# Weighted values of the attention in two TensorE passes with 128 stationary columns, in a streaming encoder step (Trainium2, one core)

## The reference, cut to what matters

```python
logits = jnp.where(mask, logits + decay, NEG)          # layer 0; layer 1 has no decay
p = jax.nn.softmax(logits, axis=-1).astype(v.dtype)
return jnp.einsum('bhqk,bkhd->bqhd', p, v)             # the weighted values
```

## Time and profile before

| what | value |
|---|---|
| median of 3 runs | 1653.4 us (1653.22 to 1656.17) |
| the profiled execution's own time | 1654.03 us |
| its span in the trace | 1652.2 us |
| PE, PEld busy | 1545.7 us (94%), 1457.5 us (88%) |
| DVE, ACT, POOL busy | 1110.3 us (67%), 727.6 us (44%), 428.2 us (26%) |
| steps of layer 0's attention | about 245 to 390 us of the span |
| steps of layer 1's attention | about 1029 to 1175 us |

### The profile page before, as it was taken

How to read it: one execution, slowest core, us unless ns; L and a number is a source line. 1 busy time by engine, 2 the same in 40 slices (tenths; PEclk the granted TensorE clock), 3 DMA queues, 4 the chain that set the end, 5 groups by cost and what they waited for, 6 DMA issues and landing times.

```text
span 1652.2 us, 30865 instructions
## 1 busy us (share of the span) xinstructions
PE 1545.7 (94%) x10826; PEld 1457.5 (88%) x10826; DVE 1110.3 (67%) x1965; ACT 727.6 (44%) x1492; POOL 428.2 (26%) x441
## 2 busy tenths in 40 slices
PE   4999979999979999999999897999987999999997
PEld 3787769998979999999998687999887999999997
DVE  4131038775878788888865236777587888888875
ACT  3312137775443343343344334777444334333424
POOL 1110024553332222222100002455233221222210
PEclk8999969999989999999999898999998999999999
DMA  7244531210121231232140447221012223312211
GB/s 261 87 137 136 150 99 49 58 40 26 52 77 54 100 102 62 90 102 71 56 144 11 170 144 209 79 64 33 26 52 77 65 89 102 102 52 101 102 51 58
DMA packets 127637, 146.06 MB, mean 88 GB/s; under 512 B 17761, under 2 KB 103841, under 8 KB 127569
## 3 DMA queue, kind: packets, MB, share of 16 engines
q1 hardware_dynamic: 127568, 145.16, 27.4%
HBM read 120.54 MB, written 24.60 MB: 88 GB/s over the span
## 4 chain that ended last, share of the span: by engine, by line
PE 80%; issue 6%; DVE 6%; ACT 3%; DMA 2%; POOL 1%; SPq 1%; POOLq 0%; DVEq 0%; ACTq 0%
PE ps L2009 26%; PE ps L1705 22%; PE ps L2040 20%; PE ps L1867 3%; PE ps L1911 2%; PE ps L1913 1%; PE ps L1912 1%; PE ps L1882 1%; PE ps L1890 1%; PE ps L1838 1%; POOL sacc L713 1%; DVE pre L1494 1%; DVE ptl L1347 1%; PE ps L1860 1%; DMA xn<-in_meta_tokens 0%
## 5 line engine op out<-in xcount | busy, mean ns | idle before, releaser
L1532 DVE TENSOR_TENSOR xT<-xT,ps 128x592 f32<-128x592 f32 (+1 forms) x256 | 194.9, 762 | 53.8 <-PE ps L2009 51.5
L814 POOL TENSOR_TENSOR ssum<-raw 128x512 f32<-128x512 f32 x32 | 43.1, 1347 | 486.2 <-DVE wul L1438 486.2
L2040 PE MATMUL ps<-bh,wuh 128*128 128x296 f32 (+1 forms) x512 | 154.5, 302 | 13.2 <-DVE wul L1438 8.2
L745 POOL TENSOR_TENSOR prob<-prob,rs 128x144 f32<-128x144 f32 (+4 forms) x160 | 118.8, 757 | 142.6 <-DVE rs L1337 142.6
L2040 PE MATMUL ps<-bl,wuh 128*128 128x296 f32 (+1 forms) x512 | 154.1, 301 | 0.0
L2040 PE MATMUL ps<-bh,wul 128*128 128x296 f32 (+1 forms) x512 | 153.8, 300 | 0.0
L1347 DVE TENSOR_TENSOR ptl<-ps,pth 128x256 fp32r<-128x256 f32 (+2 forms) x192 | 95.8, 500 | 67.8 <-ACT pth L970 67.7
L1705 PE MATMUL ps<-wh,xgh 128*128 128x512 f32 (+5 forms) x320 | 124.1, 388 | 11.5 <-issue 4.3
L1705 PE MATMUL ps<-wl,xgh 128*128 128x512 f32 (+5 forms) x320 | 122.8, 384 | 0.0
L1705 PE MATMUL ps<-wh,xgl 128*128 128x512 f32 (+5 forms) x320 | 122.6, 383 | 0.0
L2009 PE MATMUL ps<-hh,dn2h 128*128 128x296 f32 (+1 forms) x512 | 111.0, 298 | 0.0
(11 more groups left out here) (252 smaller groups left out, 4752.4 us busy)
## 6 DMA issues: line engine op xcount, KB each, us to landing
raw<-in_w_up SPq DMA_DIRECT2D x32, 1024.0 KB, 7.0
raw<-in_w_down SPq DMA_DIRECT2D x32, 1024.0 KB, 5.0
raw<-in_w_in_a SPq DMA_DIRECT2D x12, 1024.0 KB, 7.1
kv_mla<-stn SPq DMA_DIRECT2D x24, 256.0 KB, 2.2
raw<-in_w_o_a SPq DMA_DIRECT2D x8, 512.0 KB, 7.2
natk<-kv_mla SPq DMA_DIRECT2D x8, 512.0 KB, 3.5
raw<-in_w_o_b SPq DMA_DIRECT2D x8, 512.0 KB, 7.5
q_mla<-stn SPq DMA_DIRECT2D x16, 192.0 KB, 1.9
```

Of the source, the lines that this page charges most:

```text
L745: g.tensor_tensor(prob[c][0:rows, off:off + n], prob[c][0:rows, off:off + n], rs[0:rows, u:u + 1].to_broadcast([rows, n]), ALU.mult).then_ ...
L814: g.tensor_tensor(ssum[:, 1, :, :], a11, a21, ALU.subtract).then_inc(s_ready, 1)
L1532: v.tensor_tensor(a, a, two_banks(2 + m % 2, n), ALU.add).then_inc(x_ready if last else acc_done, 1)
L2040: i = te.matmul(ps[:, bank, 0:h], w[:, k, :], x, start=(u not in (3, 4, 6) and k == 0 and p == 0), stop=(k == 3 and p == 2), skip_group_ch ...
```

## The change

It joins the low and the high value tile of a head into one stationary operand of 128 columns (`vlh`, low first). One matmul of it with `pth` gives two results at once: in partitions 0 to 63 `vl*pth`, in partitions 64 to 127 `vh*pth`. A second matmul adds `vh*ptl` into partitions 0 to 63. So each block takes two matmuls instead of three, and the result lies in two halves of the partitions that still have to be added. ACT copies the upper half into `oh` as before and the lower half into a new tile `corr`; DVE subtracts `oh` from the upper half into `rest_`; POOL adds `rest_` and `corr` into `ol`, once per pair of heads over 128 partitions. ACT's and DVE's `out` move: ACT's behind `exp` 2, DVE's behind `row_max` 3. Part 0 of the weighted values waits for both copies; the copies of a pair's first head wait for POOL's addition of the pair before; `wo_first` waits for the additions instead of DVE's copies. `corr` and `rest_` lie in `sq`.

```diff
-        vh = at("vh", [P, 2, 7, P], F32R, R_G + 23552)
-        vl = at("vl", [P, 2, 7, P], F32R, R_G + 23552 + 7168)
+        vlh = at("vlh", [P, 2, 7, 2, 2, HD], F32R, R_G + 23552)
...
+        corr, rest_ = sq[:, 0, :], sq[:, 1, :]
...
+            g.memset(rst[:], 1.0).then_inc(o_sum, 1)
...
+                def add_parts(pair):
+
+                    pool.wait_ge(o_lo, pair * 2 + (H0 + 2))
+                    pool.wait_ge(o_corr, pair * 2 + (H0 + 2))
+                    g.tensor_tensor(ol[:, pair, :], rest_[:], corr[:], ALU.add).then_inc(o_sum, 1)
+
+                def head(h, c, pair=None):
+                    for u in range(4):
                         normalise(layer, h, c, u)
+                    if pair is not None:
+                        add_parts(pair)
+                    normalise(layer, h, c, 4)
...
                 for h in range(4):
-                    head(h, h % 2)
+                    head(h, h % 2, 0 if h == 3 else None)
                 with pool.Fori(0, PAIRS // 2 - 1) as i:
                     head_and_v(4 * i + 4, 0, 2 * i + 2, 0, i + 1)
-                    head(4 * i + 5, 1)
+                    head(4 * i + 5, 1, 2 * i + 1)
                     head_and_v(4 * i + 6, 0, 2 * i + 3, 1, i + 1)
-                    head(4 * i + 7, 1)
+                    head(4 * i + 7, 1, 2 * i + 2)
+                add_parts(PAIRS - 1)
...
                 def out(head, p, pair):
 
                     act.wait_ge(av_done, head + (H0 + 1))
-                    s.activation(oh[64 * p:64 * p + 64, pair, :], pf[0:HD, 3072:3072 + T],
-                                 ACT.Copy).then_inc(o_hi, 1)
+                    rows = slice(64 * p, 64 * p + 64)
+                    s.activation(oh[rows, pair, :], pf[HD:P, 3072:3072 + T], ACT.Copy).then_inc(o_hi, 1)
+                    if p == 0 and not (isinstance(pair, int) and pair == 0):
+                        act.wait_ge(o_sum, pair + (PAIRS * layer + 1))
+                    s.activation(corr[rows, :], pf[0:HD, 3072:3072 + T], ACT.Copy).then_inc(o_corr, 1)
...
-                        if u == 2 and not (isinstance(h, int) and h < 2):
-                            out(h - 2, c, pair - 1)
                         if not last:
                             qk(h, u, 1 - c)
                         exp(h, c, u)
+                        if u == 2 and not (isinstance(h, int) and h < 2):
+                            out(h - 2, c, pair - 1)
...
                     dve.wait_ge(o_hi, head + (H0 + 1))
-                    v.tensor_tensor(ol[rows, pair, :], pf[0:HD, 3072:3072 + T], oh[rows, pair, :].bitcast(F32),
+                    if p == 0 and not (isinstance(pair, int) and pair == 0):
+                        dve.wait_ge(o_sum, pair + (PAIRS * layer + 1))
+                    v.tensor_tensor(rest_[rows, :], pf[HD:P, 3072:3072 + T], oh[rows, pair, :].bitcast(F32),
                                     ALU.subtract).then_inc(o_lo, 1)
...
                     row_max(h, 2)
-                    if not (isinstance(h, int) and h < 2):
-                        out(h - 2, c, pair - 1)
                     recip(h, 1)
...
                     row_max(h, 3)
+                    if not (isinstance(h, int) and h < 2):
+                        out(h - 2, c, pair - 1)
...
                             pe.wait_ge(o_lo, head + H0)
+                            pe.wait_ge(o_corr, head + H0)
...
-                            te.matmul(out, vh[0:rows, vs, t, d], pr_h, start=(b == 0), stop=False, skip_group_check=True)
-                            te.matmul(out, vh[0:rows, vs, t, d], pr_l, start=False, stop=False, skip_group_check=True)
-                            te.matmul(out, vl[0:rows, vs, t, d], pr_h, start=False, stop=(b == 1), skip_group_check=True)
+                            te.matmul(pf[:, cols], vlh[0:rows, vs, t, p, :, :].rearrange("p s d -> p (s d)"), pr_h,
+                                      start=(b == 0), stop=False, skip_group_check=True)
+                            te.matmul(pf[0:HD, cols], vlh[0:rows, vs, t, p, 1, :], pr_l, start=False, stop=(b == 1),
+                                      skip_group_check=True)
...
-                        pe.wait_ge(o_lo, H0 + HEADS - 2)
+                        pe.wait_ge(o_sum, PAIRS * layer + PAIRS)
...
-                pe.wait_ge(o_lo, H0 + HEADS)
+                pe.wait_ge(o_sum, PAIRS * (layer + 1) + 1)
```

More of the change, by code:

```diff
@@ L230, in build @@
         op_hi, op_tmp, op_lo = sem("op_hi"), sem("op_tmp"), sem("op_lo")
+        o_corr, o_sum = sem("o_corr"), sem("o_sum")
         p_ps, snap_done, u11_done, u_add = (sem(n) for n in ("p_ps", "snap_done", "u11_done", "u_add"))
@@ L765, in split_v @@
                     src, r, t = views[0]
-                    g.tensor_tensor(vh[r, slot, NT, :].rearrange("p (h d) -> p h d", h=2), src.rearrange("p t h d -> p (t h) d"),
+                    g.tensor_tensor(vlh[r, slot, NT, :, 1, :], src.rearrange("p t h d -> p (t h) d"),
                                     ones[r, :].rearrange("p (h d) -> p h d", h=2), ALU.mult).then_inc(v_hi, 1)
                     for src, r, t in views[1:]:
-                        g.tensor_copy(vh[r, slot, t, :].rearrange("p t (h d) -> p t h d", h=2), src).then_inc(v_hi, 1)
+                        g.tensor_copy(vlh[r, slot, t, :, 1, :], src).then_inc(v_hi, 1)
                     pool.wait_ge(v_hi, j * 3 + 3 + 3 * PAIRS * layer)
@@ L772, in split_v @@
                 for src, r, t in (views[0:1] + views[2:3] if part == 1 else views[1:2]):
-                    i = g.tensor_tensor(vl[r, slot, t, :].rearrange("p t (h d) -> p t h d", h=2), src,
-                                        vh[r, slot, t, :].bitcast(F32).rearrange("p t (h d) -> p t h d", h=2), ALU.subtract)
+                    i = g.tensor_tensor(vlh[r, slot, t, :, 0, :], src, vlh[r, slot, t, :, 1, :].bitcast(F32), ALU.subtract)
                 if part == 2:
@@ L778, in attention @@
             def attention(layer):
-                def head(h, c):
-                    for u in range(5):
+                H0 = HEADS * layer
+                def add_parts(pair):
[4 more added lines that the diff above has]
+                    for u in range(4):
                         normalise(layer, h, c, u)
+                    if pair is not None:
+                        add_parts(pair)
+                    normalise(layer, h, c, 4)
                 def head_and_v(h, c, j, slot, turn):
@@ L1893, in weighted_v @@
                 def weighted_v(head, part, groups, pair, vs, p):
-                    d = slice(HD * p, HD * p + HD)
                     pe.wait_ge(g_lo, groups)
@@ L1908, in weighted_v @@
                             q0, q1 = max(first_q, P * max(b - 1, 0)), first_q + 256
-                            out = pf[0:HD, 3072 + q0:3072 + q1]
+                            cols = slice(3072 + q0, 3072 + q1)
                             pr_h, pr_l = ptv_h[0:rows, b, q0:q1], ptv_l[0:rows, b, q0:q1]
-                            te.matmul(out, vh[0:rows, vs, t, d], pr_h, start=(b == 0), stop=False, skip_group_check=True)
-                            te.matmul(out, vh[0:rows, vs, t, d], pr_l, start=False, stop=False, skip_group_check=True)
-                            te.matmul(out, vl[0:rows, vs, t, d], pr_h, start=False, stop=(b == 1), skip_group_check=True)
+                            te.matmul(pf[:, cols], vlh[0:rows, vs, t, p, :, :].rearrange("p s d -> p (s d)"), pr_h,
+                                      start=(b == 0), stop=False, skip_group_check=True)
+                            te.matmul(pf[0:HD, cols], vlh[0:rows, vs, t, p, 1, :], pr_l, start=False, stop=(b == 1),
+                                      skip_group_check=True)
                         return
                     for b, (t, rows) in enumerate(((5, P), (6, P), (NT, TX))):
-                        out = ps[0:HD, 7, 0:TX]
                         c0 = 2560 + TX * b
-                        te.matmul(out, vh[0:rows, vs, t, d], pth[0:rows, c0:c0 + TX], start=(b == 0), stop=False)
-                        te.matmul(out, vh[0:rows, vs, t, d], ptl[0:rows, c0:c0 + TX], start=False, stop=False)
-                        i = te.matmul(out, vl[0:rows, vs, t, d], pth[0:rows, c0:c0 + TX], start=False, stop=(b == 2))
+                        te.matmul(ps[:, 7, 0:TX], vlh[0:rows, vs, t, p, :, :].rearrange("p s d -> p (s d)"),
+                                  pth[0:rows, c0:c0 + TX], start=(b == 0), stop=False, skip_group_check=True)
+                        i = te.matmul(ps[0:HD, 7, 0:TX], vlh[0:rows, vs, t, p, 1, :], ptl[0:rows, c0:c0 + TX],
+                                      start=False, stop=(b == 2), skip_group_check=True)
                     i.then_inc(av_done, 1)
```

## The result

The changed kernel takes 1669.9 us (median of 5 runs, 1665.7 to 1680.1), the kernel before in the same session 1653.4 (5 runs, 1648.9 to 1656.2): ratio 1.0111, 95% interval 1.0071 to 1.0151. It is slower by 1.1%, clear of the spread of the runs. The profiled execution took 1669.92 us, its span is 1668.1 us, 15.9 more than before.

A forecast was written before the change was run, and what follows sets the result against it. It took a ring of waits through PE (some 90% loaded), ACT and DVE to bound each step. Loops -0.5 us plus tails 2 x 0.35 gave +0.2, so 1653.6 us for the median, range 1651 to 1656.5.

The forecast's parts named there:

- The failed step: ACT's two copies between `exp` 2 and `turned` 3: each was taken to cost 0.54 us, overlapping the next instruction.
- The forecast's two times, 296.98 and 297.00: Start of DVE's `turned` 3 closing a step: 296.98 in the new order, 297.00 in the old, so -0.02 us a step.
- ACT's copies cost their full length: Rival, between `exp` 2 and `turned` 3: copies don't overlap, 0.65 us each, 0.22 more a step; 1659 us, chance 0.15.
- The second miss: Rival, PE in the loops: added waits bring the granted clock to half in every third step; 1669 us, chance 0.05.
- the copy that DVE takes out of the way: DVE's copy moved behind `row_max` 3: counted, with PE's 0.47 us, as a gain that ACT's two copies take up.
- TensorE's gain: Parts 1 and 2 of the weighted values on PE: two matmuls a block instead of three save 0.47 us a step.
- the rival of the load that isn't hidden: Rival, PE's loads of 128 columns: each block pays 0.11 us more, ring closes 0.45 later; 1666 us, chance 0.05.
- DVE's wait ahead of `turned` 3: In each step, DVE idle for about 0.2 us before `turned` 3, released by ACT.
- part 0's end 0.2 us ahead of the transposes: Part 0 on PE, waiting for DVE's copy, was to end 0.15 us ahead of the end of `turned` 3.
- DVE sets the ring: Rival, loop steps: with ACT's copies under 0.42 us each, DVE decides, -0.27 us a step; 1647 us, chance 0.20.
- PE sets it all: Rival, whole loops: PE alone bounds, so its full saving of 23 us counts; 1631 us, chance 0.05.

The follow-up runs named there:

- split_high_first: Kernel split with the high part of the values in the first 64 stationary columns; 1647.76 us, ratio 0.9974 to the kernel before.
- places_back: Changed kernel with ACT's and DVE's copies back at their places before the change; 1651.32 us, ratio 1.0001 to the kernel before.
- split: Changed kernel with ACT's `oh` and DVE's copy at their old places, ACT's second copy left behind `exp` 2; 1648.76 us, ratio 0.9984 to the kernel before.
- fill: Changed kernel with the four matmuls of scores unit 4 given twice in every step; 1664.69 us, ratio 1.0085 to the kernel before.
- no_corr: Changed kernel without ACT's second copy, its terms left out of the result; 1655.41 us, ratio 1.0036 to the kernel before.
- after_free: Changed kernel, DVE's instruction reading `oh` twice, part 0 waiting for ACT's copies alone; 1668.36 us, ratio 1.0104 to the kernel before.
- dve_moved: Kernel before the change with DVE's copy alone moved behind `row_max` 3; 1664.24 us, ratio 1.0089 to the kernel before.
- act_back: Changed kernel with ACT's two copies alone back at their old place; 1671.81 us, ratio 1.0128 to the kernel before.
- best: split_high_first with the last head's low part added by DVE from PSUM, last projection taking `oh` products first; 1641.23 us, ratio 0.9936 to the kernel before.
- move_only: Kernel before the change, three passes and one ACT copy kept, both engines' copies at the new places; 1663.4 us, ratio 1.0074 to the kernel before.

## Why the prediction was wrong, step by step

*The failed step* is "A copy lasts 0.65 us and the next instruction starts about 0.11 before its end [...], so it costs 0.54". It rested on one row of an even head. After the change the way from `exp` 2 to `oh` is 0.71 us (1091.37 to 1092.08; forecast 0.58), from `oh` to the second copy 0.69 (forecast 0.54), from there to `turned` 3 0.56 (forecast 0.54, with this even head's overlap; in the next head, an odd one, 1102.71 to 1103.39, 0.68). That is 0.30 us more than in the sum in even heads and 0.42 in odd ones, and these copies are the term of the sum that was mis-sized. With the mean of the two on the forecast's step it would be 9.78 + 0.36 = 10.14; measured 10.02. The 0.1 between them is a second slip of the same kind. The forecast's two times, 296.98 and 297.00, belong to an even head's step, but its difference was set on the mean 9.80. From first transposes to first transposes (PE, before the change) an even head's step is shorter than an odd one's:

```profile
288.14 0.43 PE L1867 MATMUL ps<-cst,prob 128*128 128x128 f32 x2
...
297.81 0.43 PE L1867 MATMUL ps<-cst,prob 128*128 128x128 f32 x2
...
307.72 0.43 PE L1867 MATMUL ps<-cst,prob 128*128 128x128 f32 x2
```

The even one is 9.67 us, the odd one 9.91, for the odd head's copies lack the overlap before the change too. So the forecast for a step in the new order was really 9.67 - 0.02 = 9.65, and with the copies as measured it is 9.95 in even heads and 10.07 in odd ones, 10.01 in the mean. The rival "ACT's copies cost their full length" had the place and the price, at 0.22 us a step and a chance of 0.15, but not the cause: it thought of two engines that read the same PSUM columns, and split_high_first shows that the partitions decide. It gave 1659, and held no clock. That its 0.22 lies so near the measured 0.24 is luck: it left `oh` its overlap with the instruction ahead, and stood on the same mixed step.

*The second miss* is the clock. Nothing but the size of the waits spoke for or against it, and the rival had 0.05. It costs 5.6 us in the profiled execution. The two rivals came true together: 26 x 0.24 us and 5.6 on the forecast make 1665.4, where the changed kernel's runs begin (1665.7). As separate cases neither reached that. The rest up to the profiled execution's 1669.9 (the forecast for it was 1654.2) lies outside the loops, and no run takes it apart.

*A third step was wrong, and hidden by the first:* "the copy that DVE takes out of the way". DVE's copy was not taken out of the way. At the old place it stood where DVE has a wait anyway (for scores unit 3 at first, for `kh` once ACT has two copies there); at the new one it stands ahead of both `turned` 3 and part 0. The forecast compared the new order with the old kernel, never with the two passes in the old order, and so charged all of the loss to ACT. By the runs, in layer 1: 9.79, DVE's copy moved 10.13, ACT's too 10.17, two passes in place of three 9.75, the second copy 10.02. The other way round: two passes in the old order 9.53.

*Right:* TensorE's gain. From the start of parts 1 and 2 to the transposes behind them it was 1.65 us (298.88 to 300.53) and is 1.19 (1095.83 to 1097.02), 0.46 less, where 0.47 was forecast; with two passes the loads of PEld start like this:

```profile
1096.03 0.19 PEld L1929 LDWEIGHTS ps<-pth,vlh 128*128 128x128 f32 x1
1096.14 0.14 PEld L1931 LDWEIGHTS ps<-ptl,vlh 128*64 128x64 f32 x1
1096.26 0.19 PEld L1929 LDWEIGHTS ps<-pth,vlh 128*128 128x128 f32 x1
...
1096.50 0.19 PEld L1929 LDWEIGHTS ps<-pth,vlh 128*128 128x128 f32 x1
...
1096.67 0.19 PEld L1929 LDWEIGHTS ps<-pth,vlh 128*128 128x128 f32 x1
```

A block of 256 columns takes 0.23 to 0.24 us, one of 128 0.17 (1096.50 to 1096.67), both as forecast. So the rival of the load that isn't hidden is refuted. For these loads the rule of the Trainium skill, "TensorE: Matmul & The Clock Gate" (Part 3, The mechanism), that a load overlaps with matmuls in flight only where its row group differs, doesn't hold: loads of 0.19 us and 128 columns, on the same rows, pass every 0.23 us between matmuls that keep their pace. Right too: 352 matmuls fewer (10826 to 10474); DVE's wait ahead of `turned` 3, 0.17 us, released by ACT; part 0's end 0.2 us ahead of the transposes; POOL's addition, for which no engine waits inside the loop, is 1.46 us long (forecast 1.57); 3.03 us from the last `oh` to the projection (forecast 3.1).

*Of the other rivals:* "DVE sets the ring" and "PE sets it all" are refuted for the changed kernel, and the first is what happens in places_back and split. With TensorE's 0.46 less and the copies' orders tried here, no step fell under 9.44.

## What to carry to other kernels

Read the cost of an instruction that you move or add as the distance from start to start, over all of its variants (even and odd heads, both halves), never from one row: an overlap of 0.1 us with its neighbours can depend on where the operands lie. And set a difference on the step from which it was read, not on the mean. Before you call a moved instruction free, ask what its old place was filling, and compare each half of a change with the other half left out; here one half was worth 0.26 us a step, the other cost 0.49. And where engines wait for each other in a ring, put what every head needs (a copy out of PSUM that frees it) into the wait of its own engine, ahead of the chain, not behind it.

## What the runs showed of the hardware

- *Overlap hangs on the start partition.* ACT's copies of 64x592 overlap by 0.10 to 0.12 us with their neighbours, DVE's by about 0.08. It is lost (start 0.02 to 0.03 us behind the end) where the place that is read or written changes between partition 0 and 64. "VectorE: DVE Perf Modes" (Two Vector instructions with no wait between them) of the Trainium skill has the rule for VectorE, as a model: an instruction waits until all earlier ones have finished if one of its inputs starts in another group of 32 partitions than the first input of the last instruction that read the same memory (SBUF or PSUM), or its output in another than the last output into that memory. The DVE copies agree, also in that it counts each memory by itself: in split `recip` overlaps with the copy that read PSUM from partition 64, and `kl` behind it doesn't. ACT's copies follow the same pattern, of which the page says nothing. By it the second copy in odd heads stands alone on both sides, and the prediction's 0.54 would have been 0.68; I hadn't weighed it.
- *The clock falls in a loop of short waits.* In the changed kernel TensorE idles 0.64 us ahead of part 0 and some tenths ahead of the transposes in every step of 10.0 us, and in layer 0 of the profiled execution the granted clock was 0.76 in the mean from 358 to 372 us, a stretch that holds both of its levels, 1.2 and 2.4 GHz. The same steps in layer 1 kept 1.00, and in no kernel here did the clock fall in layer 1's loop. With steps of the same length and more matmuls in them (fill), the loops kept the clock. It also fell in layer 0's loop of no_corr, after_free, dve_moved and act_back, but not in the loops of before, places_back, split, best and move_only (one profiled execution each). The Trainium skill, "TensorE: Matmul & The Clock Gate" (A second HAM failure mode), has frequent short waits between groups of matmuls as such a cause, and fill agrees. What decides in which steps it falls, and why in layer 0 alone, is open.
